# Branch ends of a two-block transformer kernel: the row factor as a diagonal matrix in the transposing products, VectorE's h blocks first, the first two weight chunks together, and MLP ups two ahead of the downs

## The reference

```
mod = silu(c) @ w_ada + b_ada                       # six vectors of 1024 a layer: shift, scale, gate, twice
h   = rms_norm(x, norm_attn) * (1 + sc1) + sh1
x   = x + g1 * hybrid_mixer(h, w_in, w_out, rel_bias)      # two kinds of attention, 8 heads each
h   = rms_norm(x, norm_ffn) * (1 + sc2) + sh2
x   = x + g2 * peer_ffn(h, wq, sub_keys, u_emb, v_emb)     # product keys, 16384 experts, all computed
x   = rms_norm(x, norm_final)
for i in range(2):                                  # block two, ada_w[i], norm_g[i]
    h = rms_norm(x, g[i,0]) * (1 + sc1) + sh1
    y = nsa_mixer(h) if i == 0 else swa_sink_mixer(h)
    x = x + (1 + g1) * rms_norm(y, g[i,1])
    h = rms_norm(x, g[i,2]) * (1 + sc2) + sh2
    y = relu(h @ w_up[i])**2 @ w_down[i]            # 1024 -> 4096 -> 1024
    x = x + (1 + g2) * rms_norm(y, g[i,3])
```

## Time and profile before

| | before |
|---|---|
| runs | 1739.90, 1740.66, 1741.63 us; median 1740.66 |
| profiled execution: span | 1736.1 us |
| profiled execution's own time | not listed apart from the runs; the runs' median is 4.56 us over the span |
| PE busy | 1675.0 us (96%) |
| DVE, ACT, POOL busy | 1232.2, 915.4, 513.6 us |
| mean granted clock of PE | 0.98 of full speed |
| weights and inputs read | 337.9 MB |

### The profile page before, as it was taken

The page is one execution under the profiler, slowest core; times in us unless marked ns, Lnnn a source line. Parts: engine busy times, 40 slices in busy tenths (PEclk is TensorE's granted clock), DMA queues, the critical chain, the costliest instruction groups (busy, mean ns, idle before and its releaser), DMA issues.

```text
span 1736.1 us, 31849 instructions
## 1 busy us (share of the span) xinstructions
PE 1675.0 (96%) x11010; PEld 1480.3 (85%) x11010; DVE 1232.2 (71%) x2231; ACT 915.4 (53%) x1753; POOL 513.6 (30%) x207
## 2 busy tenths in 40 slices
PE   6998999999999999999999999998999999799998
PEld 3966899999999998788888879965899999489997
DVE  5467759689719893877777858846788877656666
ACT  3454544455469994455555555358544445564443
POOL 0961128989875546000000004500200006020000
PEclk9999999999999999999999998989999999899999
DMA  8865655565553334988888655440477764045553
GB/s 335 316 221 195 257 177 182 181 181 182 181 170 119 113 109 160 328 289 290 289 289 287 223 181 150 141 156 1 158 273 276 285 210 143 13 133 184 191 183 109
DMA packets 98424, 341.11 MB, mean 196 GB/s; under 512 B 12147, under 2 KB 16003, under 8 KB 98340
## 3 DMA queue, kind: packets, MB, share of 16 engines
q1 hardware_dynamic: 93988, 336.01, 56.9%
q10 hardware_dynamic: 4352, 4.02, 0.8%
HBM read 337.87 MB, written 1.07 MB: 195 GB/s over the span
## 4 chain that ended last, share of the span: by engine, by line
PE 86%; DVE 5%; ACT 4%; DMA 2%; issue 1%; ACTq 0%; SPq 0%; DVEq 0%
PE banks L644 25%; PE banks L645 25%; PE banks L646 25%; PE banks L985 3%; PE banks L830 1%; PE banks L797 1%; DVE arena L1686 1%; DMA ada_ring<-in_ada 1%; DVE arena L2149 1%; DMA arena<-in_ada 1%; ACT arena L1321 1%; PE banks L846 1%; ACT weights_high L1279 1%; PE banks L715 1%; PE banks L775 1%
## 5 line engine op out<-in xcount | busy, mean ns | idle before, releaser
L600 POOL TENSOR_TENSOR weights_low<-ring,weights_high 128x1024 fp32r<-128x1024 f32 x202 | 512.4, 2550 | 1017.7 <-DVE ht_low L1761 584.7
L1279 ACT ACTIVATE weights_high<-ring 128x1024 fp32r<-128x1024 f32 x480 | 505.8, 1055 | 481.5 <-PE banks L646 475.2
L644 PE MATMUL banks<-ht_high,weights_high 128*128 128x256 f32 x2016 | 583.1, 289 | 3.9 <-DVE ht_low L1761 3.7
L645 PE MATMUL banks<-ht_low,weights_high 128*128 128x256 f32 x2016 | 572.4, 284 | 0.0
L646 PE MATMUL banks<-ht_high,weights_low 128*128 128x256 f32 x2016 | 572.2, 284 | 0.0
L644 PEld LDWEIGHTS banks<-ht_high,weights_high 128*128 128x128 f32 x2016 | 388.8, 193 | 10.1 <-issue 6.1
L645 PEld LDWEIGHTS banks<-ht_low,weights_high 128*128 128x128 f32 x2016 | 388.9, 193 | 2.7
L646 PEld LDWEIGHTS banks<-ht_high,weights_low 128*128 128x128 f32 x2016 | 388.4, 193 | 0.0
L1741 DVE TENSOR_TENSOR weights_low<-ring,weights_high 128x1024 fp32r<-128x1024 f32 x278 | 339.6, 1223 | 44.4 <-ACT weights_high L1279 38.8
L644 PE MATMUL banks<-weights_high,ga_parts 128*128 128x512 f32 x504 | 197.5, 392 | 6.9 <-DVE ga_parts L2061 6.9
L645 PE MATMUL banks<-weights_low,ga_parts 128*128 128x512 f32 x504 | 196.8, 391 | 0.0
(11 more groups left out here) (287 smaller groups left out, 2252.5 us busy)
## 6 DMA issues: line engine op xcount, KB each, us to landing
ring<-in_stream SPq DMA_DIRECT2D x490, 512.0 KB, 3.6
arena<-in_ada SPq DMA_DIRECT2D x88, 512.0 KB, 4.8
ada_ring<-in_ada SPq DMA_DIRECT2D x56, 512.0 KB, 4.4
arena<-bias_rows ACTq DMA_DIRECT2D x1, 2048.0 KB, 16.4
X<-in_x SPq DMA_DIRECT2D x1, 1024.0 KB, 6.2
out<-X SPq DMA_DIRECT2D x4, 256.0 KB, 2.0
arena<-arena ACTq DMA_DIRECT2D x8, 127.5 KB, 6.0
arena<-in_norm_final SPq DMA_DIRECT2D x1, 512.0 KB, 4.6
```

Of the source, the lines that this page charges most:

```text
L600: pool.tensor_tensor(WL[:, c % SLOTS, :], ring[:, c % SLOTS, :], WH[:, c % HIGHS, :], ALU.subtract)\
L644: pe.matmul(out, wh, xh, start=start, stop=False, **kw)
L645: pe.matmul(out, wh, xl, start=False, stop=False, **kw)
L1279: act.activation(WH[:, c % HIGHS, :], ring[:, c % SLOTS, :], ACT.Copy).then_inc(S["high_ready"], 1)
```

## The change

It touches the six branch ends and the order within the MLPs:

- `norm` no longer scales 128x1024 by the row factor. It makes `rdiag`, the identity times the row factor (128x128), and `norm_transpose` multiplies each block of X (ZN at n=2) by it: a matmul in place of a transpose.
- DVE makes h blocks 0 and 1, ACT blocks 2 to 7, and the first chunk takes them in the order 0, 2, 1, 3, ..., 7.
- `first_pair`: at n=1 to 5 the first two chunks are multiplied together, block by block; four products with the high of h, then a wait for its low, then two. Their results lie in the two halves of bank 7.
- `keep_busy(6)` becomes `keep_busy(2)`.
- The lows of chunks `first + 1` and `first + 2` are made by POOL at n=1, 3, 5 and `first + 1` at n=2, 4, where DVE had them.
- In the MLPs the ups are two ahead of the downs, in PE, ACT, DVE and the host's order of the stream.
- `product` calls what it has between chunks 0, 1 and 2 after chunk 2; at n=0 DVE waits for the constants before its first norm.

```
-BY_DVE = [FIRST_CHUNK[name] + i for name, first, n in [("qk1", 0, 2), ("wq", 0, 16), ("v", HIGHS, NKEYS + 2), ("out2", 0, HIGHS), ("mlp2", 0, 64 + 2),
-                                                    ("mlp3", 0, 64)] for i in range(first, n)]
+BY_DVE = [FIRST_CHUNK[name] + i for name, first, n in [("qk1", 0, 2), ("wq", 0, 1), ("wq", 3, 16), ("v", HIGHS, NKEYS + 1), ("out2", 0, HIGHS),
+                                                    ("mlp2", 0, 1), ("mlp2", 3, 64 + 1), ("mlp3", 0, 1), ("mlp3", 3, 64)]
+          for i in range(first, n)]
...
+BLOCK_ORDER = [0, 2, 1, 3, 4, 5, 6, 7]
+DVE_BLOCKS = [0, 1]
+ACT_BLOCKS = [b for b in range(DB) if b not in DVE_BLOCKS]
...
-                pool.wait_ge(S["ht_by_dve"], 12 * (n + 1))
+                pool.wait_ge(S["ht_low"], DB * (n + 1))
             pool.wait_ge(S["low_by_dve"], 2)
             lows(2, chunk["wq"])
+            lows(chunk["wq"] + 1, chunk["wq"] + 3)
...
             lows(chunk["out2"] + HIGHS, chunk["mlp2"])
+            lows(chunk["mlp2"] + 1, chunk["mlp2"] + 3)
+            low(chunk["swa"] + 1)
             split_done(4)
             lows(chunk["swa"] + 2, chunk["mlp3"])
+            lows(chunk["mlp3"] + 1, chunk["mlp3"] + 3)
...
-                return banks[:, 6 + n % 2, 0:T]
-
-            def product(name, n, rhs, ready, between=lambda m: None):
-                for m in range(n):
-                    chunk_blocks(chunk[name] + m, out_bank(OUTS[name] + m), rhs, ready=None if m else ready)
-                    between(m)
+                return out_home(n)
+
+            def first_pair(c, o, norm):
+
+                ws = [arrived_split(c + i) for i in range(2)]
+                pe.wait_ge(S["out_taken"], o)
+                outs = [out_home(o + i) for i in range(2)]
+                for i, k in enumerate(BLOCK_ORDER):
+                    wait_high(norm, k)
+                    for n, (wh, wl) in enumerate(ws):
+                        pe.matmul(outs[n], wh[:, k * P:(k + 1) * P], HTH[:, k, :], start=i == 0 and n == 0, stop=False, skip_group_check=True)
+                        pe.matmul(outs[n], wl[:, k * P:(k + 1) * P], HTH[:, k, :], start=False, stop=False, skip_group_check=True)
+                    pe.wait_ge(S["ht_low"], DB * norm + i + 1)
+                    for n, (wh, wl) in enumerate(ws):
+                        m = pe.matmul(outs[n], wh[:, k * P:(k + 1) * P], HTL[:, k, :], start=False, stop=i == DB - 1, skip_group_check=True)
+                        if i == DB - 1:
+                            m.then_inc(S["chunk_used"], 1)
+
+            def product(name, n, rhs, norm, between=lambda m: None):
+                first_pair(chunk[name], OUTS[name], norm)
+                for m in range(2, n):
+                    chunk_blocks(chunk[name] + m, out_bank(OUTS[name] + m), rhs)
+                    for i in range(m + 1) if m == 2 else [m]:
+                        between(i)
...
                     for b in range(DB):
-                        m = pe.transpose(xt(n, b)[:, tile[t]],
-                                         (XN2 if n in (2, 3) else XN)[:, t, b * P:(b + 1) * P], ident)
+                        m = pe.matmul(xt(n, b)[:, tile[t]], (ZN if n == 2 else X)[:, t, b * P:(b + 1) * P], rdiag[:, t, :],
+                                      start=True, stop=True)
...
-            keep_busy(6, 13 - SUM_BANK[2])
+            keep_busy(2, 13 - SUM_BANK[2])
...
-                up(c0, o0, ready=lambda k: h_ready(norm, k))
+                first_pair(c0, o0, norm)
                 for j in range(4):
-                    up(c0 + 1 + 2 * j, o0 + 1 + j)
-                    down(c0 + 2 + 2 * j, j, first=j == 0)
+                    up(c0 + 2 + 2 * j, o0 + 2 + j)
+                    down(c0 + 3 + 2 * j, j, first=j == 0)
                 with pe.Fori(0, 6) as r:
                     for j in range(4, 8):
-                        up(c0 + 1 + 2 * j, o0 + 1 + j, more=r * 4)
-                        down(c0 + 2 + 2 * j, j, more=r * 4)
-                for j in range(29, 32):
+                        up(c0 + 2 + 2 * j, o0 + 2 + j, more=r * 4)
+                        down(c0 + 3 + 2 * j, j, more=r * 4)
+                for j in range(30, 32):
...
-                dst, src = XN2 if k in (3, 4) else XN, ZN if k == 3 else X
-                dve.tensor_scalar(dst[:, t, :], src[:, t, :], small[:, 32 + t:33 + t], None, ALU.mult)\
-                    .then_inc(S["xn_ready"], 1)
+                dve.tensor_scalar(rdiag[:, t, :], ident, small[:, 32 + t:33 + t], None, ALU.mult).then_inc(S["xn_ready"], 1)
...
-                for b in (6, 7):
+
+                def block(b):
                     dve.wait_ge(S["xt_ready"], DB // 2 * n + b // 2 + 1)
                     dve.tensor_scalar(HT[:, b, :], xt(n, b), scl[:, n, b:b + 1],
                                       mod[:, v, b:b + 1], ALU.mult, ALU.add).then_inc(S["ht_by_dve"], 1)
-                for b in (6, 7):
-                    dve.wait_ge(S["ht_by_dve"], 12 * n + b - 5)
-                    dve.tensor_copy(HTH[:, b, :], HT[:, b, :]).then_inc(S["ht_by_dve"], 1)
-
-                for b in range(DB):
-                    if b < 6:
-                        dve.wait_ge(S["hth_by_act"], 6 * n + b + 1)
+
+                def high(b):
+                    i = 2 * n + DVE_BLOCKS.index(b) + 1
+                    dve.wait_ge(S["ht_by_dve"], i)
+                    dve.tensor_copy(HTH[:, b, :], HT[:, b, :]).then_inc(S["hth_by_dve"], 1)
+
+                def rest(b):
+                    if b in DVE_BLOCKS:
+                        dve.wait_ge(S["hth_by_dve"], 2 * n + DVE_BLOCKS.index(b) + 1)
                     else:
-                        dve.wait_ge(S["ht_by_dve"], 12 * n + 4)
-                    dve.tensor_tensor(HTL[:, b, :], HT[:, b, :], HTH[:, b, :], ALU.subtract).then_inc(S["ht_by_dve"], 1)
+                        dve.wait_ge(S["hth_by_act"], 6 * n + ACT_BLOCKS.index(b) + 1)
+                    dve.tensor_tensor(HTL[:, b, :], HT[:, b, :], HTH[:, b, :], ALU.subtract).then_inc(S["ht_low"], 1)
+                block(0)
+                high(0)
+                rest(0)
+                block(1)
+                rest(2)
+                high(1)
+                rest(1)
+                for b in range(3, DB):
+                    rest(b)
...
-                low(first + 1)
                 shift_banks(3 + k)
                 if k != 1:
-                    low(first + 2)
+                    low(first + 3)
```

More of the change, by code:

```diff
@@ L297, in two_blocks @@
         epsc = sb("epsc", [P, 1])
+        rdiag = sb("rdiag", [P, TT, P])
         ones_row = sb("ones_row", [1, 60])
@@ L450, in two_blocks, with out_home @@
         ROPE2, ROPE3 = len(ROPES2), len(ROPES3)
+        PAIRED = [OUTS[name] for name in ("wq", "nsa", "up2", "swa", "up3")]
+        def out_home(n):
+            if n - 1 in PAIRED:
+                return banks[:, 7, T:2 * T]
+            return banks[:, 7 if n in PAIRED else 6 + n % 2, 0:T]
         block = ctx.enter_context(nc.Block())
@@ L618, in _ @@
             lows(chunk["v"], chunk["v"] + HIGHS)
+            low(chunk["nsa"] + 1)
             split_done(2)
@@ L649, in columns_of, with chunk_blocks @@
                 return w[0][:, lo:lo + n], w[1][:, lo:lo + n]
-            def chunk_blocks(c, out, rhs, more=0, ready=None, middle=None):
+            def chunk_blocks(c, out, rhs, more=0, middle=None):
                 w = arrived_split(c, more)
                 for k in range(DB):
-                    if ready:
-                        ready(k)
                     if middle and k == DB // 2:
@@ L903, in _ @@
             out = out_bank(OUTS["qk1"])
[L904 to L907, removed]
+            for i, k in enumerate(BLOCK_ORDER):
+                wait_high(0, k)
+                pe.wait_ge(S["ht_low"], i + 1)
+                passes(out, columns_of(w, k * P, P), h_rhs(k), i == 0, i == DB - 1)
+                m = passes(banks[0:68, 4, 0:T], (WIKH[:, k, :], WIKL[:, k, :]), h_rhs(k), i == 0, i == DB - 1)
             m.then_inc(S["chunk_used"], 1)
@@ L1069, in between @@
                         beside[m]()
-                product(name, n, h_rhs, lambda k: h_ready(norm, k), between)
+                product(name, n, h_rhs, norm, between)
                 for m in (n - 1,):
@@ L1216, in _ @@
             norm_transpose(5, lambda: summed_3(ADA_BEFORE["mlp2"] + 4 * DB, (15, 16), 10))
[L1217 removed]
+            keep_busy(2, 13 - SUM_BANK[10])
             mlp("3", 5)
@@ L1308, in take @@
                     used(chunk[name] + m)
-                    o = OUTS[name] + m
-                    act.activation(dst(m), banks[:, 6 + o % 2, 0:T], func, scale=scale(m)).then_inc(S["out_taken"], 1)
+                    pair_done(OUTS[name] + m, chunk[name])
+                    act.activation(dst(m), out_home(OUTS[name] + m), func, scale=scale(m)).then_inc(S["out_taken"], 1)
                     between(m)
@@ L1568, in _ @@
                         act.wait_ge(S["rope_done"], last_unit[m - 3] + 1)
```

(29 more changed lines are left out.)

61 lines of the change are left out of this document (35 added, 26 removed).

## The result

The changed kernel takes 1749.3 us (median of 4, 1745.86 to 1752.15), the kernel before 1740.28 in the runs beside it (median of 4): 1.0057 times, 95% interval 1.0039 to 1.0075. Timed again as e9 it takes 1749.27, 1.0059 times (1.0042 to 1.0076). It was to be 1738.8, in 1734.0 to 1744.0. Beside the experiments the kernel before has medians of 1738.4 to 1739.8. Two single executions lie far outside all others, one of e8 (2071.75 us) and one of e14 (5293.45); medians and ratios hardly feel them.

A forecast was written before the change was run, and what follows sets the result against it. PE, busy 1675.0 of 1736.1 us, was taken to set the time. Changes at ends n=1 to 5 (-0.1, -1.7, +0.3, -0.1, -0.3) summed to -1.9 us: 1740.66 to 1738.8, range 1734.0 to 1744.0.

The forecast's parts named there:

- T1: At each branch end, the start of the second tile's eight transposing products.
- D: Time from T1 to the end of the second chunk; claimed 8.1 us at full clock if the h blocks keep ahead.
- calls between chunks that run after the third: Calls that product now makes after the third chunk; claimed to cost nothing.
- Half the stretch's cost: Ends n=1 to 4: half of a half-clock stretch's cost counted; a whole one costs 1.7 us, 5 at n=2.
- n=2, -1.7: End n=2: -0.5 at T1, -3.7 for D, +2.5 for half clock; range -4.2 to +0.8 us.
- The doubling, +0.86 a tile: Each end's transposing products: 16 passes for eight transposes, 0.93 us to 1.79 a tile.
- The hold, +1.5 at T1: n=3 and n=5: POOL's early lows hold DVE's bias too, delaying T1 by 1.5 us; the middle of three cases.
- in between the halves: Case at n=5: POOL's low gets in between the two halves of DVE's residual, L2204; T1 +2.15 us.
- Rival C: POOL's lows don't hold DVE before T1; n=3 0.8 and n=5 1.05 us lower; -3.7, 1737.0 us; chance 0.18.
- range of n=1: End n=1: forecast -0.1 us, between -1.0 and +0.8.
- Rival A: Clock stays at 2.4 GHz at all ends, as plain products replace transposes; -6.5, 1734.2 us; chance 0.20.
- Rival B: Half-clock stretch on useful work, the pair of chunks, at every end; +4.5, 1745.2 us; chance 0.16.

The follow-up runs named there:

- e9: The changed kernel itself, unaltered, timed again in a later group of runs: 1749.27 us, 1.0059 of before.
- e8: The changed kernel with n=2's first two chunks one after the other and the calls between chunks where before had them: 1745.85 us, 1.0038 of before.
- e14: The changed kernel with the first chunks' lows back on DVE for wq, nsa and swa (n=1, 2 and 4) alone: 1748.18 us, 1.0048 of before.
- e6: e5 with the pair undone at n=2 alone and the calls between chunks where before had them: 1735.23 us, 0.998 of before.
- e5: The changed kernel with transposes and DVE's scaling back and the first chunks' lows on DVE: 1737.3 us, 0.9995 of before.
- e2: The changed kernel with the lows of the first chunks back on DVE, as before: 1742.39 us, 1.0028 of before.
- e3: The kernel before with the diagonal and plain products alone (and n=0's wait for constants): 1748.9 us, 1.0053 of before.
- e1: The changed kernel with the transposes and DVE's 128x1024 scaling back: 1742.25 us, 1.0028 of before.
- e13: The changed kernel with the first chunks' lows back on DVE for mlp2 and mlp3 (n=3 and n=5) alone: 1740.81 us, 1.0008 of before.
- e12: e6 with no keep_busy at n=1, 3, 4 and 5: 1738.22 us, 1.0002 of before.
- e11: e6 with six keep_busy products in place of two: 1735.35 us, 0.9979 of before.
- e4: The changed kernel with keep_busy(6) in place of keep_busy(2) at all four places: 1751.76 us, 1.007 of before.

## Why the prediction was wrong

Lengths of the profiles less those of before, by the prediction's steps (us; forecast, the changed kernel, e9):

| | forecast | changed | e9 |
|---|---|---|---|
| n=0 | 0 | +2.7 | +0.2 |
| n=1 | -0.1 | +0.5 | +0.5 |
| n=2 | -1.7 | +2.0 | +0.4 |
| stage behind n=2 | 0 | +4.5 | +4.6 |
| n=3 | +0.3 | +1.1 | +2.5 |
| n=4 | -0.1 | -0.6 | +1.5 |
| n=5 | -0.3 | +2.2 | +2.1 |
| other stages | 0 | +1.8 | -0.5 |
| sum | -1.9 | +14.2 | +11.3 |

Split at T1, the five ends say which terms failed. Up to T1 they take 4.0 us more in the changed kernel's profile (4.2 in e9), and the sum had +3.9. D takes 1.3 us more (2.9 in e9), and the sum had -5.8: with 7.1 us this is the largest of its errors. The stage behind n=2, n=0 and the other stages, all at nothing, are 4.5, 2.7 and 1.8 us longer in the changed kernel's profile, but only the first of these came again in e9.

- **"calls between chunks that run after the third", at nothing: failed.** I named no cover for it. The rotations were what it moved, with three buffers behind them and POOL's lows on top; 4.2 us a profile, 3.4 in the medians (e8), 2.1 without the other costs (e6 against e5). My own showed DVE held in just that stage, and I used them for n=3 and n=5 only.
- **D of 8.1 us: failed by the clock, the step that weighed most.** The pair itself does what the sum says: its 48 products take 5.94 us at n=3 (1264.98 to 1270.92), where I had 5.84, and DVE's lows keep ahead of them. But the half-clock stretch stays at n=1 and n=3 and comes to n=5 (in e9 to n=4 too), and now it lies on products that count: the 16 plain products at T1 take 3.4 to 3.8 us at n=1, 2, 3 and 5, not 1.79 (at n=4, at full clock, 2.03 with the last one's latency). With the clock as it came the sum's D holds: 3.4 us at half clock make 8.1 into 9.8 at n=1 and n=3, where 9.70 was measured, and 5.2 us make it 10.7 at n=5, measured 10.54. "Half the stretch's cost" was the wrong middle. Where the clock is full and DVE isn't held, in e2 at n=3, it is 8.42 us from T1 (1253.81) to the third chunk (1262.23), near the sum's 8.1.
- **n=2, -1.7: wrong in sign.** A full clock was worth 3.7 us there, of which I kept 1.2. The clock fell (0.58 for 0.61), and the second tile's doubled products took 3.76 us. This end varies most: it lasts 16.5 to 22.6 us in the nine profiles that pair there and 19 to 22.6 in the seven that don't, longest where D has the most half clock, so one profile says little about it.
- **The doubling, +0.86 a tile: right as a size at full clock, too small in effect.** e3 shows +10 us for it alone, and e1 -7. Twelve tiles of 0.9 us are 10.7 us; I had let most of this vanish in the waits for DVE, in DMA time at n=0 (1.7 us not hidden), and in D, where it sat on the path. n=0 moving by more than 0.5 us was one of my signs of being wrong.
- **The hold, +1.5 at T1: there, and right in size by luck.** T1 came 1.63 us later (T0, the start of the first tile's products, to T1 +1.96, and the first tile 0.33 sooner). But it was the case "in between the halves", which I had costed at +2.15, and not the middle one that I took: DVE was held 2.10 us (3.51 for 1.41), and `rdiag` gave 0.47 back (0.28 for 0.75), together the 1.63. What I didn't have is the half clock that came with it: e13 puts both together at 5.1 us, where the sum had 0.8 + 1.05 = 1.85. By the Trainium skill's rule of the shared port pair (SBUF — State Buffer, Who interferes with whom), a VectorE instruction with two SBUF inputs contends with a GpSimd one that reads SBUF. The trace agrees: L2261, L2205 and L2207, with operands in SBUF alone, are held (3.51 us for two, 2.45 and 2.14), and L2206 with one in PSUM is not (0.41).
- **Rival C fell:** POOL's low got in between DVE's two halves at n=3 and n=5, and PE waited 1.30 and 1.15 us for `rdiag`.
- **n=4, -0.1, MLPs at nothing, range of n=1:** right in the changed kernel's profile. PE waits 0.95 us for POOL's third low at n=4, as forecast, and the MLPs last 173.80 and 179.84 us for 173.91 and 179.93.
- **Rival A fell, and the rule that spoke for it.** By the Trainium skill (TensorE: Matmul & The Clock Gate, Part 4: PE-mode transpose) transpose mode doesn't count as busy as products do. Here plain products, twice as many, raised the clock of no end but n=1, and there from 0.83 to 0.85 (e3), and the changed kernel has the same mean clock with them as with transposes (e1), 0.9755 over the runs of each.
- **Rival B had the sign, not the size or the place alone.** Its sign at n=5 came (a clock of 0.75), but 4.5 us were half of the loss: half clock also lay on the products at T1, ahead of B's place, and the stage behind n=2 was at nothing in B too.

## What to carry to other kernels

An edit "at nothing" needs its cover named as much as any: here a call order cost 2 to 4 of the 9 us lost, through a buffer ring three instructions away. Where PE is nearly full, a plain f32 product in place of a transpose has its price: here it is two passes for one, and at an end they are on the path. And when moving work from DVE to POOL, list DVE's SBUF-only operations that fall into POOL's time; keep the ones before a PE wait out of it.

## What the runs showed of the hardware that I had not expected

Half clock came where PE had waited, and also where it hadn't. At the rotations of the changed kernel it began 0.3 us after the end of a wait of 1.80 us (1087.01), but in e9 the same wait of 1.80 us (1081.16) was followed by a clock of 1.00. At n=5 it began 0.4 us ahead of the wait for `rdiag`, and in e13, without that wait, it still takes 3.4 us of D. So the runs show that n=3 and n=5 had more half clock with a held DVE (3.4 to 6.8 us each in seven profiles, 0 to 3.4 in e2 and e13), not that a wait brings it.

No filler instead of two cost 3 us (e12). Six instead of two cost nothing where PE would be idle (e11); where it wasn't, they came out 2.5 us slower, which is not clear of noise (e4). Executions of one kernel differ by up to 0.6%, and with them the mean clock: in e9 1744.17 us at 0.981 and 1754.79 us at 0.970.
